# Summing two parts of a weight product's columns in the same accumulating transfers

## The chip, the cores and the metric

The kernel runs on one core of one Trainium2 chip. The metric is the time of one execution in device microseconds (us); lower is better.

## The reference, cut to what matters

Two transformer layers of width 1024 over 512 tokens. The attention halves differ; the part that matters here is the feed-forward half, which both layers have in the same shape:

```python
D_FF = -(-8 * D_MODEL // (3 * 256)) * 256        # 2816
hn = rms_norm(h, ffn_norm_g[l])
h = h + (jax.nn.silu(hn @ w_ffn_gate[l]) * (hn @ w_ffn_up[l])) @ w_ffn_down[l]
```

Everything is float32. `w_ffn_gate` and `w_ffn_up` are 1024 x 2816: 22 column tiles of 128 each.

## The kernel before, in words

Every product is done in three passes of reduced-precision matmuls: ScalarE rounds a weight tile (`wh`, the high part, `high`, L918), VectorE or GpSimd subtracts to get the rest (`wl`, the low part, L1398 and `low`, L746), and TensorE multiplies high by high, high by low and low by high (`product`, L2293).

The inner width 2816 is worked in three parts of 8, 6 and 8 column tiles (`FPARTS`). A part is first multiplied by gate and up (`gu1a`, `gu1b`, `gu1c`), then by its rows of the down weights (`dn1a` and so on); layer 2 has the same with `gu2a` to `dn2c`. In the first part four tiles of each of gate and up are plain products (`GATE_PLAIN`). All others are done in pairs of tiles with seven half products in place of eight (`tile_pair`, L2316), a scheme of the Strassen kind. Such an entry (one pair of tiles of gate, or of up) needs the weights' rows and columns in sums: four blocks of 512 rows of the weights added or copied in DRAM, `weight_sums_*`, two tensors per weight. The entries of a part are one gate and one up entry for each pair: 4 entries in part a, 6 in part b, 8 in part c.

Who makes the sums: GpSimd (POOL), in `sum_dmas`. For each layer and each part there are 16 transfers from DRAM to DRAM over the part's columns: numbers 0 to 7 are plain copies (issued at L769), 8 to 15 are accumulating ones (`accum_op=add`, L771), which read and add to what the copies left. Each transfer has 512 rows; a row is as wide as the part's pairs: 2 pairs (1024 bytes) in part a, 3 pairs (1536 bytes) in part b and 4 pairs (2048 bytes) in part c. All of them count on one semaphore, `sums_in`. In part a POOL waits only at numbers 8, 12 and 14. From part b's number 8 on (`16 * part + n >= 24`), so also at part c's copies, it waits before every transfer for all that went before, so that one is in flight at a time.

When: POOL works its own instructions in order. In layer 1 it issues part a's 16 between its `low` work for the gates (`SUMS_AT[1]`), part b's copies between the bias units of the latent attention (`mask_bias`, every fourth), and then `feed_sums` waits until the branches are mixed (`mix_ok`, L818) and issues numbers 8 to 15 of part b and all 16 of part c. In layer 2 ten of part b's 16 go between the gates, and `feed_sums` issues its other six and the 16 of part c.

Who reads them: SyncE (SP) issues the weight loads in order of use. Before the entries of a part it waits on `sums_in` for that part's sums (L672). For an entry (`load_pair`) it issues four loads: a 512 KB one of the first columns (L595, waits for `lo[0]`), a 512 KB one of a sum tensor (`wsum`, L605), a 256 KB one of the second columns (L607, waits for `lo[1]` of the entry before), and a 512 KB one of the other sum tensor (L611). All these loads have rows of 512 bytes. ScalarE then makes the high parts in its own order: `sum_high` (L1166) and `second_high` (L1172) stand in that order between the copies of the entry's partial products (`part_x`, L1226 and L1237; `part_z`), for which TensorE waits. The down tiles are loaded in two halves each (L619).

Of the kernel before, what the change touches and what calls it, by code (L numbers as in the profile page):

```python
# [39 lines left out]
FPARTS = (8, 6, 8)  # L40
# [52 lines left out]
GATE_PLAIN = (4, 0, 0)  # L93
# [15 lines left out]
def pair_list(l, part):  # L109

    return [e for i, n in gate_pairs(l, part) for e in ((i, 2 * n, False), (i + 1, 2 * n + 1, True))]
# [10 lines left out]
def first_pair(part):  # L122

    return sum(FPARTS[:part]) // 2


def tile_col(part, i):

    return (first_pair(part) + i // 2 + FPAIRS * (i % 2)) * P
# [4 lines left out]
    return i // 2 + FPARTS[part] // 2 * (i % 2)  # L134


def summed_pairs(part):

    return first_pair(part) + GATE_PLAIN[part] // 2, first_pair(part) + FPARTS[part] // 2


def down_before(l, part):
# [2 lines left out]


SUM_DMAS = 16
SUMS_AT = {1: (0, 2, 4, 6, 8, 10, 12, 14, 16), 2: (8, 10, 12, 14, 16, 19, 22, 24, 26)}


PHASES = [("kv1", 4, KD, 1), ("bq1", 2, KD, 1), ("iq1", 2, KD, 1), ("aq1", 4, KD, 2), ("uq1", 4, 2, 1),
# [150 lines left out]
def build(nc, t, out):  # L302
    with ExitStack() as ctx:
        def sem(name):
            return ctx.enter_context(nc.semaphore(name))
# [263 lines left out]
        sums_in, ws_hi, ws_lo = [sem(n) for n in "sums_in ws_hi ws_lo".split()]  # L569
# [10 lines left out]
        def by_rows(w, k0=0, kc=None):  # L580
            v = w.rearrange("(k p) n -> p k n", p=P)
            return v if kc is None else v[:, k0:k0 + kc, :]
# [5 lines left out]
        def _(sp):  # L588
            def load(name, i, b, src, col, piece=0, width=P):

                kc = KC[name]
                slot = stage[:, b, 0:kc * P].rearrange("p (k n) -> p k n", k=kc)
                if piece == 0 and not (name == "kv1" and isinstance(i, int) and i == 0):
                    sp.wait_ge(lo[b], PAIR0[name] + i)
                sp.dma_start(slot[:, :, piece:piece + width], src[:, :, bass.ds(col, width)]).then_inc(w_in[b], 16)  # L595
# [57 lines left out]
            def layer_rest(l, win, gates_at, wa, wb, wo, wg, wu, wd):  # L653
                if l == 1:
                    sp.wait_ge(lo[0], PAIR0["gates1"])
                    sp.dma_start(stage[:, 0, 0:2 * P].rearrange("p (k n) -> p k n", n=P), win[:, 0:2, gates_at:gates_at + P]).then_inc(w_in[0], 16)
                    load("gates1", 0, 1, win, gates_at + P)
                with sp.Fori(2 - l, PAIRS[f"gates{l}"]) as i:
                    for b in range(2):
                        load(f"gates{l}", i, b, win, i * (2 * P) + (gates_at + b * P))  # L660
                with sp.Fori(0, PAIRS[f"br{l}"]) as i:
                    load(f"br{l}", i, 0, by_rows(wa), i * P)
                    load(f"br{l}", i, 1, by_rows(wb), i * P)
                with sp.Fori(0, PAIRS[f"out{l}"]) as i:
                    for b in range(2):
                        load(f"out{l}", i, b, by_rows(wo), i * (2 * P) + b * P)
                for part, ab in enumerate("abc"):
                    f0 = sum(FPARTS[:part])
                    for i in range(GATE_PLAIN[part]):
                        load(f"gu{l}{ab}", i, 0, by_rows(wg), tile_col(part, i))  # L670
                        load(f"gu{l}{ab}", i, 1, by_rows(wu), tile_col(part, i))
                    sp.wait_ge(sums_in, 16 * SUM_DMAS * (3 * l - 3 + part + 1))  # L672
                    for i, q, up in pair_list(l, part):
                        load_pair(f"gu{l}{ab}", i, q, l, "u" if up else "g", first_pair(part) + (i - up) // 2)
                    with sp.Fori(0, PAIRS[f"dn{l}{ab}"]) as i:
                        for b in range(2):
                            load_down(f"dn{l}{ab}", i, b, wd, part)
# [30 lines left out]
        def _(pool):  # L708
# [40 lines left out]
                low(name, i, 0)  # L749
                low(name, i, 1)  # L750

            def sum_dmas(l, part, first, last):

                before = SUM_DMAS * (3 * l - 3 + part)
                t0, t1 = summed_pairs(part)
                cols = slice(t0 * P, t1 * P)
                second = slice((FPAIRS + t0) * P, (FPAIRS + t1) * P)
                upper, lower = slice(0, D // 2), slice(D // 2, D)
                for n in range(first, last):
                    if before + n and (n in (0, 8, 12, 14) or 16 * part + n >= 24):  # L760
                        pool.wait_ge(sums_in, 16 * (before + n))
                    m = "gu"[n % 2]
                    w, s12, s43 = w_ffn[l, m], w_sums[l, m, 0], w_sums[l, m, 1]
                    to, src = ((s12[upper, cols], w[upper, second]), (s43[lower, cols], w[upper, cols]),
                               (s12[lower, cols], w[lower, second]), (s43[upper, cols], w[lower, cols]),
                               (s12[upper, cols], w[lower, second]), (s43[lower, cols], w[upper, second]),
                               (s12[lower, cols], s43[lower, cols]), (s43[upper, cols], s12[lower, cols]))[n // 2]
                    if n < 8:
                        pool.dma_start(to, src).then_inc(sums_in, 16)  # L769
                    else:  # L770
                        pool.dma_start(to, src, accum_op=ALU.add).then_inc(sums_in, 16)  # L771

            def copies(row, dram, length, h0, h1):

                pool.dma_start(dram[:, h0:h1, 0:length], row[h0:h1].unsqueeze(0).broadcast_to([P, h1 - h0, length])).then_inc(f_out, 16)
# [18 lines left out]
            for i in range(PAIRS["gates1"]):  # L796
                if 2 <= i < 6:
                    pool.wait_ge(f_out, 16 * i)
                    windows(fB_dram, LEN_B, biasB, NKEY, 2 * i - 4, 2 * i - 2, biasB_in)
                if 1 <= i < 5:  # L800
                    copies(fB_row, fB_dram, LEN_B, 2 * i - 2, 2 * i)
                if i == 0:
                    low("gates1", i, 1)
                else:
                    low_pair("gates1", i)
                sum_dmas(1, 0, SUMS_AT[1][i], SUMS_AT[1][i + 1])

            def mask_bias(j):

# [6 lines left out]
            def feed_sums(l):  # L816

                pool.wait_ge(mix_ok, KD * l)  # L818
                sum_dmas(l, 1, 8 if l == 1 else 10, SUM_DMAS)
                sum_dmas(l, 2, 0, SUM_DMAS)  # L820

            la_units = list(latent_units())
            for b in range(2):
# [1 line left out]
            pool.wait_ge(biasB_in, 4 * 16)  # L825
            for j in range(len(la_units)):
                mask_bias(j)
                if j % 4 == 3:
                    sum_dmas(1, 1, j // 4, j // 4 + 1)

            feed_sums(1)

# [64 lines left out]
            sum_dmas(2, 0, 7, 8)  # L897
            for i in range(PAIRS["gates2"]):
                low_pair("gates2", i)
                part = SUMS_AT[2][i] // SUM_DMAS  # L900
                sum_dmas(2, part, SUMS_AT[2][i] - part * SUM_DMAS, SUMS_AT[2][i + 1] - part * SUM_DMAS)
            feed_sums(2)


# [2020 lines left out]
```

## Time and profile before

| | us |
|---|---|
| median of 3 runs (lowest, highest) | 1473.24 (1470.36, 1475.11) |
| the profiled execution's own time | 1473.38 |
| its span | 1471.7 |
| PE busy | 1452.7 (99%) |
| DVE busy / ACT busy / POOL busy | 975.2 / 654.3 / 258.2 |
| DMA queue of SP / of POOL, share of the 16 engines | 36.4% / 24.8% |

PE is TensorE's matmuls, PEld its weight loads, DVE VectorE, ACT ScalarE, POOL GpSimd, SP SyncE; a q behind a name is the engine's sequencer. The time of an execution is its span and 1.7 us around it. The granted TensorE clock is at its full 2.4 GHz level all along.

### The profile page before, as it was taken

The numbers are of one execution on the slowest core, as the hardware profiler recorded it, in microseconds if no ns is written. First come the engines' busy times: TensorE is split into PE (matmuls) and PEld (weight loads), VectorE is DVE, ScalarE is ACT, GpSimd is POOL, SyncE is SP. The second block draws the span as 40 slices with busy tenths as digits, with TensorE's granted clock in tenths as the row PEclk, the third lists the DMA queues.
The fourth block names the chain that finished last, engine by engine and source line by source line (L and its number), as shares of the span: only waits on it lengthen the run. The fifth ranks groups of instructions, "written<-read, shape, count | busy, mean of one in ns | idle before, by whom it ended". The sixth has DMA issues, their size and how long they took to land.

```text
span 1471.7 us, 23871 instructions
## 1 busy us (share of the span) xinstructions
PE 1452.7 (99%) x8712; PEld 1253.2 (85%) x8712; DVE 975.2 (66%) x1779; ACT 654.3 (44%) x1175; POOL 258.2 (18%) x260
## 2 busy tenths in 40 slices
PE   9999999999999999999999999999999999999998
PEld 8868786888898898999899777777888988989997
DVE  6678977575776576787744372434767765867875
ACT  5234446535453353465411373544344533534643
POOL 2024536201101100000003675331011001000000
PEclk9999999999999999999999999999999999999999
DMA  7536674249899993663223237653388999736632
GB/s 187 148 100 211 173 133 130 79 111 191 202 328 226 250 217 98 199 184 106 86 86 86 58 101 162 151 188 80 107 186 226 305 218 242 213 95 195 185 104 93
DMA packets 342909, 236.91 MB, mean 161 GB/s; under 512 B 24729, under 2 KB 322837, under 8 KB 342814
## 3 DMA queue, kind: packets, MB, share of 16 engines
q1 hardware_dynamic: 305518, 152.24, 36.4%
q0 software_dynamic: 37216, 83.27, 24.8%
q8 instruction: 60, 0.98, 0.3%
q14 instruction: 35, 0.29, 0.1%
q10 hardware_dynamic: 80, 0.14, 0.0%
HBM read 233.48 MB, written 81.88 MB: 214 GB/s over the span
## 4 chain that ended last, share of the span: by engine, by line
PE 88%; DMA 6%; DVE 3%; ACT 1%; issue 1%; DVEq 0%; SPq 0%; POOL 0%; ACTq 0%
PE psL L2293 37%; PE psL L2520 12%; PE psS L2316 10%; PE psL L2316 6%; PE psS L2293 5%; PE psT L2316 4%; PE psT L2529 2%; DMA stage<-in_w_ffn_up 1%; DMA stage<-in_w_ffn_gate 1%; DMA stage<-in_w_ff_up 1%; PE psL L2655 1%; PE psS L2836 1%; PE psS L2570 1%; PE psL L2791 1%; PE psS L2814 1%
## 5 line engine op out<-in xcount | busy, mean ns | idle before, releaser
L918 ACT ACTIVATE wh<-stage 128x1024 fp32r<-128x1024 f32 (+3 forms) x211 | 203.6, 965 | 362.1 <-PE psL L2293 199.6
L1398 DVE TENSOR_TENSOR wl<-stage,wh 128x1024 fp32r<-128x1024 f32 (+2 forms) x168 | 183.8, 1094 | 57.7 <-ACT wh L918 57.3
L2293 PE MATMUL psL<-hid,wh 128*128 128x512 f32 x672 | 207.3, 390 | 0.0
L2520 PE MATMUL psL<-hn,wh 128*128 128x512 f32 x496 | 165.0, 414 | 0.8 <-DVE yn L2176 0.8
L2293 PE MATMUL psL<-hn,wh 128*128 128x512 f32 x528 | 165.0, 394 | 0.0
L2293 PEld LDWEIGHTS psL<-hid,wh 128*128 128x128 f32 x672 | 125.6, 188 | 26.2 <-DVE wl L1398 0.6
L2293 PE MATMUL psL<-hid,wl 128*128 128x512 f32 x336 | 130.7, 389 | 0.0
L746 POOL TENSOR_TENSOR wl<-stage,wh 128x1024 fp32r<-128x1024 f32 (+1 forms) x43 | 97.7, 2273 | 172.7 <-ACT wh L918 172.7
L2293 PEld LDWEIGHTS psL<-hn,wh 128*128 128x128 f32 x528 | 97.7, 188 | 23.1 <-issue 3.3
L2520 PEld LDWEIGHTS psL<-hn,wh 128*128 128x128 f32 x496 | 84.5, 189 | 24.5 <-issue 11.1
L2293 PE MATMUL psL<-hn,wl 128*128 128x512 f32 x264 | 102.9, 390 | 0.0
L1901 DVE TENSOR_TENSOR wsl<-wsum,wsh 128x1024 fp32r<-128x1024 f32 x72 | 88.2, 1224 | 22.3 <-ACT wsh L1166 21.4
L2520 PE MATMUL psL<-hn,wl 128*128 128x512 f32 x248 | 97.8, 394 | 0.0
L2316 PE MATMUL psS<-xt,wsh 128*128 128x256 f32 x432 | 80.2, 283 | 0.8 <-ACT part_x L1226 0.8
L2293 PE MATMUL psL<-mix,wh 128*128 128x512 f32 x256 | 79.9, 393 | 0.8 <-DVE wl L1814 0.8
L2293 PE MATMUL psS<-hn,wh 128*128 128x264 f32 x416 | 78.5, 290 | 0.9 <-DVE hn L1845 0.5
L1166 ACT ACTIVATE wsh<-wsum 128x1024 fp32r<-128x1024 f32 x72 | 75.4, 1048 | 5.6 <-DMA wsum<-weight_sums_1g 1.9
L2293 PEld LDWEIGHTS psL<-hid,wl 128*128 128x128 f32 x336 | 63.1, 188 | 13.2
L2028 DVE TENSOR_TENSOR ft<-psL,Rk 128x512 f32<-128x512 f32 x46 | 31.8, 691 | 62.4 <-PE psL L2293 62.4
L2316 PEld LDWEIGHTS psS<-xt,wsh 128*128 128x128 f32 x432 | 67.4, 192 | 1.0 <-ACT part_x L1226 1.0
L2293 PEld LDWEIGHTS psS<-hn,wh 128*128 128x128 f32 x416 | 65.7, 192 | 2.6 <-issue 1.2
L2316 PE MATMUL psS<-xt,wsl 128*128 128x256 f32 x216 | 61.1, 283 | 0.0
(507 smaller groups left out, 3333.0 us busy)
## 6 DMA issues: line engine op xcount, KB each, us to landing
stage<-in_w_in SPq DMA_DIRECT2D x53, 512.0 KB, 4.0
wsum<-weight_sums_1g SPq DMA_DIRECT2D x18, 512.0 KB, 5.2
wsum<-weight_sums_1u SPq DMA_DIRECT2D x18, 512.0 KB, 5.3
wsum<-weight_sums_2g SPq DMA_DIRECT2D x18, 512.0 KB, 4.7
wsum<-weight_sums_2u SPq DMA_DIRECT2D x18, 512.0 KB, 4.5
stage<-in_w_out SPq DMA_DIRECT2D x16, 512.0 KB, 4.7
stage<-in_w_ffn_down SPq DMA_DIRECT2D x32, 256.0 KB, 3.0
stage<-in_w_ff_down SPq DMA_DIRECT2D x32, 256.0 KB, 3.0
```

Source lines behind the costliest of these rows:

```text
L746: pool.tensor_tensor(wl[:, b, 0:n], stage[:, b, 0:n], wh[:, b, 0:n].bitcast(F32), ALU.subtract).then_inc(lo[b], 1)
L918: act.activation(wh[:, b, 0:n], stage[:, b, 0:n], ACT.Copy).then_inc(hi[b], 1)
L1166: act.activation(wsh[:, cols], wsum[:, cols], ACT.Copy).then_inc(ws_hi, 1)
L1398: v.tensor_tensor(wl[:, b, 0:n], stage[:, b, 0:n], wh[:, b, 0:n].bitcast(F32), ALU.subtract).then_inc(lo[b], 1)
L1901: v.tensor_tensor(wsl[:, cols], wsum[:, cols], wsh[:, cols].bitcast(F32), ALU.subtract).then_inc(ws_lo, 1)
L2028: v.tensor_tensor(ft[:, 2 * b, :], psL[:, b, :], R, ALU.mult).then_inc(upper_ok, 1)
L2293: ins = pe.matmul(dst, w[:, b, k * P:(k + 1) * P], x[:, part, k, c0:c1], start=done_ + n == 0, stop=done_ == kc - 1 and n == 2)
L2316: ins = pe.matmul(dst, w[:, cols], x(part, k), start=not add and k + n == 0, stop=k == KD // 2 - 1 and n == 2, skip_group_check=True)
L2520: ins = pe.matmul(psL[:, b, :], w[:, b, k * P:(k + 1) * P], hn[:, part_, k, META:], start=k + n == 0, stop=k == KD - 1 and n == 2)
L2529: ins = pe.transpose(psT[:, n % 2, m * P:(m + 1) * P], tile[:, col:col + P], ident[:])
L2570: ins = pe.matmul(psS[:, 2 * (i % 2) + 1, h * HD:(h + 1) * HD], PTa[:, u % 2, n * P:(n + 1) * P], avn[:, c, h // 4 * HD:h // 4 * HD + HD], ...
L2655: ins = pe.matmul(psL[:, i % 2, h * HD:(h + 1) * HD], PT[:, n % 4, m * P:(m + 1) * P], vB[:, c, h * HD:(h + 1) * HD], start=h == 0 and m = ...
```

## The change

Each layer's sums are now made in two chunks instead of three: chunk 0 is part a's two pairs as before, chunk 1 is the three pairs of part b and the four of part c together, in 16 transfers whose rows are seven pairs (3584 bytes) wide. There are 32 transfers per layer instead of 48, for the same bytes. Where they stand in POOL's order changes with them: in layer 1 chunk 0's and the first two copies of chunk 1 go between the gates, the other six copies between the bias units 3, 8, 13, 18, 23 and 28, and `feed_sums` issues numbers 8 to 15; in layer 2 copies 0 to 5 go between the gates, and `feed_sums` issues copies 6 and 7 and the accumulating 8 to 15. SP waits for all of chunk 1 before part b's first entry.

```diff
+CHUNK_OF = (0, 1, 1)
+def summed_pairs(chunk):
+    parts = [n for n, c in enumerate(CHUNK_OF) if c == chunk]
+    return first_pair(parts[0]) + GATE_PLAIN[parts[0]] // 2, first_pair(parts[-1] + 1)
-SUMS_AT = {1: (0, 2, 4, 6, 8, 10, 12, 14, 16), 2: (8, 10, 12, 14, 16, 19, 22, 24, 26)}
+SUM_CHUNKS = max(CHUNK_OF) + 1
+SUMS_AT = {1: (0, 3, 6, 8, 10, 12, 14, 16, 18), 2: (8, 10, 12, 14, 16, 17, 19, 20, 22)}
+SUMS_LATER = {n: 5 * n - 7 for n in range(2, 8)}
...
-                    sp.wait_ge(sums_in, 16 * SUM_DMAS * (3 * l - 3 + part + 1))
+                    sp.wait_ge(sums_in, 16 * SUM_DMAS * (SUM_CHUNKS * (l - 1) + CHUNK_OF[part] + 1))
...
-                    if before + n and (n in (0, 8, 12, 14) or 16 * part + n >= 24):
+                    if before + n and (n in (0, 8, 12, 14) or chunk and n >= 8):
                         pool.wait_ge(sums_in, 16 * (before + n))
...
+            def sums_due(l, i):
+                for n in range(SUMS_AT[l][i], SUMS_AT[l][i + 1]):
+                    sum_dmas(l, n // SUM_DMAS, n % SUM_DMAS, n % SUM_DMAS + 1)
...
-                sum_dmas(1, 0, SUMS_AT[1][i], SUMS_AT[1][i + 1])
+                sums_due(1, i)
...
                 pool.wait_ge(mix_ok, KD * l)
-                sum_dmas(l, 1, 8 if l == 1 else 10, SUM_DMAS)
-                sum_dmas(l, 2, 0, SUM_DMAS)
+                sum_dmas(l, 1, 8 if l == 1 else 6, SUM_DMAS)
...
                 mask_bias(j)
-                if j % 4 == 3:
-                    sum_dmas(1, 1, j // 4, j // 4 + 1)
+                for n, unit in SUMS_LATER.items():
+                    if unit == j:
+                        sum_dmas(1, 1, n, n + 1)
...
-                part = SUMS_AT[2][i] // SUM_DMAS
-                sum_dmas(2, part, SUMS_AT[2][i] - part * SUM_DMAS, SUMS_AT[2][i + 1] - part * SUM_DMAS)
+                sums_due(2, i)
```

## Rows read from the trace of the kernel before

**Rows 1.** The page: engines' busy time, and the two large DMA queues.
```profile
PE 1452.7 (99%) x8712; PEld 1253.2 (85%) x8712; DVE 975.2 (66%) x1779; ACT 654.3 (44%) x1175; POOL 258.2 (18%) x260
...
q1 hardware_dynamic: 305518, 152.24, 36.4%
q0 software_dynamic: 37216, 83.27, 24.8%
```
**Rows 2.** Waits of PE's weight loads, 500 to 545 us: total, times, longest.
```profile
PEld psL L2316 <- ACT part_x L1226: 3.9, 2, 2.4
PEld psS L2316 <- ACT part_x L1226: 1.0, 1, 1.0
```
**Rows 3.** The same for 1160 to 1200 us.
```profile
PEld psL L2316 <- ACT part_x L1237: 0.7, 1, 0.7
PEld psL L2316 <- ACT part_x L1226: 0.6, 1, 0.6
PEld psT L2316 <- DVE wsl L1901: 0.6, 1, 0.6
```
**Rows 4.** Chain that ended last, from part a (layer 1) on: start, length, what.
```profile
415.85 10.07 PE psS L2316 x84
...
501.63 10.32 DMA stage<-in_w_ffn_up
...
513.36 11.18 DMA stage<-in_w_ffn_gate
...
524.56 0.64 ACT wh L1172
...
525.23 0.70 DVE wl L1906
```
**Rows 5.** POOL in order of time, layer 1: start, length [idle before, releaser].
```profile
327.69 1.05 POOL L771 DMA_DIRECT2D weight_sums_1g<-in_w_ffn_gate  x1 [60.38 <-DVE mix L1822]
...
396.07 0.66 POOL L769 DMA_DIRECT2D weight_sums_1g<-in_w_ffn_gate  x1 [8.89 <-DMA weight_sums_1u<-weight_sums_1u]
...
452.18 1.04 POOL L771 DMA_DIRECT2D weight_sums_1g<-in_w_ffn_gate  x1 [6.96 <-DMA weight_sums_1u<-in_w_ffn_up]
...
499.91 1.01 POOL L771 DMA_DIRECT2D weight_sums_1u<-weight_sums_1u  x1 [7.77 <-DMA weight_sums_1g<-weight_sums_1g]
512.05 1.01 POOL L771 DMA_DIRECT2D weight_sums_1g<-weight_sums_1g  x1 [11.12 <-DMA weight_sums_1u<-weight_sums_1u]
524.66 1.01 POOL L771 DMA_DIRECT2D weight_sums_1u<-weight_sums_1u  x1 [11.60 <-DMA weight_sums_1g<-weight_sums_1g]
```
**Rows 6.** DMA packets and queues in four stretches of 1 us: 382, 374, 508 and 512.
```profile
DMA packets 128, 0.20 MB, mean 197 GB/s; under 512 B 0, under 2 KB 128, under 8 KB 128
...
DMA packets 206, 0.21 MB, mean 210 GB/s; under 512 B 0, under 2 KB 206, under 8 KB 206
...
DMA packets 165, 0.21 MB, mean 209 GB/s; under 512 B 0, under 2 KB 84, under 8 KB 165
...
DMA packets 683, 0.35 MB, mean 348 GB/s; under 512 B 4, under 2 KB 683, under 8 KB 683
```
**Rows 7.** SP in order of time, layer 1: start, length.
```profile
408.60 0.37 SPq L607 DMA_DIRECT2D stage<-in_w_ffn_gate  x1
...
443.04 38.71 SPq L619 DMA_DIRECT2D stage<-in_w_ffn_down  x16
486.17 0.38 SPq L595 DMA_DIRECT2D stage<-in_w_ffn_gate  x1
```
**Rows 8.** The load issued at 417.33 and the one at 370.07: KB, us to landing.
```profile
stage<-in_w_ffn_up SPq DMA_DIRECT2D x1, 256.0 KB, 7.2
...
stage<-in_w_ffn_gate SPq DMA_DIRECT2D x1, 512.0 KB, 8.2
```
**Rows 9.** POOL in order of time, layer 2.
```profile
1068.59 1.00 POOL L771 DMA_DIRECT2D weight_sums_2g<-in_w_ff_gate  x1 [52.39 <-DVE mix L1822]
...
1174.54 1.04 POOL L771 DMA_DIRECT2D weight_sums_2g<-in_w_ff_gate  x1 [7.38 <-DMA weight_sums_2u<-in_w_ff_up]
```
**Rows 10.** SP in order of time, layer 2.
```profile
1148.43 0.37 SPq L607 DMA_DIRECT2D stage<-in_w_ff_gate  x1
...
1229.15 0.38 SPq L595 DMA_DIRECT2D stage<-in_w_ff_gate  x1
```
**Rows 11.** The copy of part b's sums issued at 239.08: KB, us to landing.
```profile
weight_sums_1g<-in_w_ffn_gate POOLq DMA_DIRECT2D x1, 768.0 KB, 4.6
```

More of the change, by code:

```diff
@@ L134, in hid_slot @@
     return i // 2 + FPARTS[part] // 2 * (i % 2)
-def summed_pairs(part):
-    return first_pair(part) + GATE_PLAIN[part] // 2, first_pair(part) + FPARTS[part] // 2
+CHUNK_OF = (0, 1, 1)
+def summed_pairs(chunk):
+    parts = [n for n, c in enumerate(CHUNK_OF) if c == chunk]
+    return first_pair(parts[0]) + GATE_PLAIN[parts[0]] // 2, first_pair(parts[-1] + 1)
 def down_before(l, part):
@@ L750, in low_pair, with sum_dmas @@
                 low(name, i, 1)
-            def sum_dmas(l, part, first, last):
-                before = SUM_DMAS * (3 * l - 3 + part)
-                t0, t1 = summed_pairs(part)
+            def sum_dmas(l, chunk, first, last):
+                before = SUM_DMAS * (SUM_CHUNKS * (l - 1) + chunk)
+                t0, t1 = summed_pairs(chunk)
                 cols = slice(t0 * P, t1 * P)
```

## The prediction

> **What bounds the kernel now.** I read the page first: PE is busy 99% of the span [rows 1], so a transfer matters only where PE waits for what it brings, and the whole idle time of PE is 1471.7 - 1452.7 = 19.0 us. Then I asked for the waits of PE's weight loads in the stretches of the feed-forward parts. Late weights cost PE something in two places: 3.9 + 1.0 = 4.9 us in layer 1 between 500 and 545 us, in part b [rows 2], and 0.7 + 0.6 + 0.6 = 1.9 us in layer 2 between 1160 and 1200 us, in part a [rows 3]. Part a of layer 1, part b of layer 2 and both parts c have none worth naming. So 6.8 us is all that the change can win from the transfers it merges.
>
> Why the 4.9 us arise is to be seen by laying the chain beside POOL's order. The second loads of three entries are issued at 501.63, 513.36 and 525.95, each 1.3 to 1.7 us after an accumulating transfer of four pairs (499.91, 512.05, 524.66), and take 10.3, 11.2 and 10.2 us, as long as that transfer [rows 4, 5]. The high and the low part follow (0.64 and 0.70 us), and only then does the next entry's second load go out. So an entry took as long as an accumulate, about 12.0 us, where PE needs 10.07 [rows 4]. The packets in single microseconds tell why a load waits [rows 6]: with no accumulate active the loads move 683 packets of 512 bytes in 1 us; beside an accumulate of four pairs they move 84 to its 81, and beside one of three pairs (206 packets, 210 GB/s, which solves to 104 to 102) again one to one. Alone, rows of three pairs go at 128 in 1 us.
>
> **The change, part by part.**
>
> The accumulates. 128 rows of 1536 bytes in 1 us over 16 engines is 125 ns a row and engine; a load packet in between adds 16/683 us = 23 ns. A transfer of 512 rows is 32 per engine: three pairs 32 x (125 + 23) = 4.7 us of active time, four pairs 32 x (167 + 23) = 6.1 us, seven pairs 32 x (292 + 23) = 10.1 us, an estimate that scales the row by its bytes. The rest of a transfer's period is latency at both ends in which loads run freely. In the feed-forward stretch the periods before are (396.07 - 327.69)/8 = 8.5 us for three pairs, and 12.0 us for four pairs beside entries [rows 5]. Seven pairs then take 8.5 + 5.4 = 13.9 us beside plain tiles and 12.0 + 4.0 = 16.0 us beside entries. Bounds from rows: at least 8.5 us a transfer (if width cost nothing), at most 8.5 x 7/3 = 19.9 us (if all of it grows with the bytes).
>
> When they run. Layer 1: from 327.69 on, five at 13.9 reach 397, three at 16.0 end at 445. Before, the three-pair ones ended at 396, copies of four pairs ran to 452.18 and the four-pair accumulates from there to 536 [rows 5]. So part b loses its accumulates and its 4.9 us stall goes; but part a, whose loads go out from 403 to 443 [rows 7], now meets accumulates with the long active time where it met copies. Layer 2: from 1068.59 [rows 9] two copies of seven pairs, 14 us as an estimate from two of 4.6 us at three pairs [rows 11] scaled by 7/3 with loads between them, little of it overlapped, then five at 13.9 to 1152 and three at 16.0 to 1200. Part a's second loads go out from 1148.43 on [rows 10], so its four entries lie under the fifth to the eighth.
>
> What one costs part a. An entry's four loads are 1.75 MB, 3584 packets. In a period of 16.0 us the loads get 512 packets in the active 10.1 us and 683 x 5.9 = 4030 outside it: 4540, good for 1.27 entries or 12.7 us of PE. That is a loss of 3.3 us each at the least, if the loads use every gap. If the entries lock to the accumulates as they did in part b before, one entry goes with each: a loss of 16.0 - 10.1 = 5.9 us. I take the middle, 4.6. Against it stands the slack at part a: the load issued at 417.33 took 7.2 us [rows 8] and was there at 424.5, and ACT needs it about 1 us behind the entry's start at 425.9 (the first start at 415.85 and one entry more), so about 2.5 us, spent once in each layer. The accumulate that covers the first entry is absorbed by SP's lead, since that entry's loads go out 7 us ahead of it. Layer 1: 2 x 4.6 - 2.5 = 6.7 (4.1 to 9.3). Layer 2: 3 x 4.6 - 2.5 = 11.3 (7.4 to 15.2).
>
> Plain tiles (out, and the first of gate and up). A load issued just behind a three-pair accumulate takes 8.2 us [rows 8] with no stall; with seven pairs it is 8.2 + 5.4 = 13.6 us. A load can be issued about three tiles ahead of its use (5.4 us each), less rounding and subtracting twice: some 11.7 us. Only a load in the first 2 us of a transfer can be late, one in three. I take 0, with 2.4 us a layer as the other end.
>
> The wait moved at L672. SP comes to it when the down loads of part a are out, at 443.04 + 38.71 = 481.8, and its next load goes at 486.17 [rows 7]; chunk 1 is there at 445. In layer 2 the load is at 1229.15 [rows 10] and the chunk at 1200. 0 us; behind this wait stand all of part b's loads, so it is the dearest place if the chunk is late (a rival below).
>
> POOL. Sixteen issues less per layer. In the attention phases two issues of 0.63 us fewer stand between the bias units; PE's own work ends the waits there, so 0. The wider copies there run beside few loads; the 60 us [rows 5] for which POOL then idles is their cover. Copies between the gates: same cover. If that were gone, a copy's extra 3 us would have to be seen in a gate tile's load, which has two tiles' time.
>
> Sum: 1473.4 + 6.7 + 11.3 - 4.9 - 1.9 = 1484.6 us, against a profiled time that is the median of the runs within 0.2 us.
>
> Two rules of the Trainium skill bear on this, both on its page "DMA: Bandwidth & Descriptors". The rows show packets of the two queues alternating one to one [rows 6]; the section "Queues, rings and completion order" says that an engine takes turns between queues by packets, whatever a packet holds, which speaks against wide rows beside narrow ones, and by it the sum stands as above. The section "Anatomy of one DMA — SWDGE (gpsimd) path" gives 2.0 us fixed and the bytes at 436 GB/s, by which 1.8 MB would take 6.2 us and merging would be a clear gain; the trace does not agree for accumulates, whose rows move at 197 GB/s when alone [rows 6].
>
> **Rivals.**
>
> A, faster: the accumulates need not grow so much, the gaps carry part a's loads, and the stalls of before go. For it: nothing is in flight beside part b any more, and part a of layer 1 had no stall. Against it: one-to-one packets. If seven pairs took 8.5 to 12 us each, no entry would be late: 1473.4 - 6.8 = 1466.6 us; with a us or two left in each layer 1468.
>
> B, no change: the entries' stalls only move from part b to part a, about 3 us in each layer, since the loads catch up in gaps and slack is larger than I read: 1473 us, 1470 to 1477.
>
> C, slower by another way: chunk 1 is late at SP's wait. It decides from 19.9 us a transfer on: layer 1 would end at 327.7 + 159 = 487, 1 us late and covered, layer 2 at 1068.6 + 14 + 159 = 1242, 12.5 us behind 1229.15, of which some 7 are covered by SP's lead. That is 6 us on top of part a's loss at its upper ends (9.3 + 15.2 + 4.8 - 6.8 = 22.5): 1501 us.
>
> **How the numbers follow.** Forecast (part a pays, 1478 to 1496) 0.5; A 0.22; B 0.2; C 0.08. The forecast's own range is the lower bounds, 1473.4 + 11.5 - 6.8 = 1478, to the upper, 1496. For the range of 8 in 10 I go down to 1467, which takes in B and most of A, and up to 1495. A measurement of this kernel tells 0.3%, 4.4 us, from no change. Faster: A, with a little of B, 0.24. Same: most of B and the edges of its neighbours, 0.22. Slower: 0.54.
>
> **What would show it.** Right: accumulates of chunk 1 with periods of about 14 and then 16 us, ending near 445 (later by the stalls) and 1200; PE waiting for `part_x` in part a of both layers, 6.7 and 11.3 us; load packets at some 50 in 1 us while one is active; no waits left in layer 1's part b. Wrong: periods under 12 us, or part a without stalls, which gives A; a gap in SP behind the last down load of part a, which gives C. PE waits in the out and plain tiles would show the term that I set to 0.

## The result and the profile after

| | before | after |
|---|---|---|
| median of 4 runs (lowest, highest), us | 1471.8 (1467.6, 1475.1) | 1517.1 (1515.1, 1519.5) |
| span of the profiled execution | 1471.7 | 1517.8 |
| PE busy / PE idle in the span | 1452.7 / 19.0 | 1468.9 / 48.9 |
| mean granted clock | 0.997 | 0.986 |

The changed kernel takes 1.0308 times as long (95% interval 1.0283 to 1.0334): slower, as forecast, but by 45 us where 11 were forecast, and outside the range.

The page after, the lines that answer to [rows 1]:
```profile
PE 1468.9 (97%) x8712; PEld 1262.9 (83%) x8712; DVE 977.8 (64%) x1779; ACT 655.9 (43%) x1175; POOL 231.8 (15%) x228
q1 hardware_dynamic: 305518, 152.24, 35.1%
q0 software_dynamic: 25696, 83.27, 22.9%
```
The same 8712 matmuls now take 16.2 us more, so part of the loss is the clock, and PE stands still 29.9 us more. Both DMA queues move the same bytes as before.

The difference lies in few stages. I cut the spans where PE's first matmul of each stage starts and asked for the busy time in each. Columns of a row: stretch, its length, then busy time of PE, PEld, DVE, ACT, POOL, and at the end the granted clock, the DMA share and GB/s. Before, plain tiles (out, first gate and up) and part a's entries of layer 1, part b's entries, then plain tiles and part a of layer 2:
```profile
326.10:415.70 89.60, 89.60 (x395) 73.11 (x396) 62.06 (x88) 40.55 (x53) 10.67 (x12) 1.00 0.92 210
415.70:456.00 40.30, 40.30 (x338) 40.30 (x336) 30.12 (x42) 22.59 (x39) 3.55 (x5) 1.00 0.96 297
499.60:566.50 66.90, 62.69 (x506) 62.08 (x504) 46.48 (x63) 33.84 (x58) 3.04 (x3) 0.97 0.84 211
1067.00:1156.60 89.60, 89.60 (x394) 73.09 (x395) 62.27 (x88) 40.45 (x53) 9.89 (x12) 1.00 0.89 227
1156.60:1199.00 42.40, 41.17 (x338) 40.53 (x338) 29.87 (x42) 22.25 (x38) 4.33 (x5) 1.00 1.00 257
```
After, the same five:
```profile
325.90:433.20 107.30, 96.62 (x394) 76.76 (x395) 61.88 (x88) 40.85 (x53) 8.11 (x8) 0.94 1.01 212
433.20:480.30 47.10, 43.03 (x338) 42.80 (x337) 30.91 (x43) 22.81 (x39) 0.00 (x0) 0.93 0.63 176
523.80:584.30 60.50, 60.50 (x505) 60.46 (x505) 47.22 (x63) 34.19 (x58) 0.00 (x0) 1.00 0.58 166
1084.60:1192.80 108.20, 95.87 (x395) 75.98 (x396) 61.52 (x88) 40.75 (x53) 8.38 (x9) 0.95 0.99 226
1192.80:1245.10 52.30, 43.63 (x337) 43.23 (x336) 31.03 (x43) 22.71 (x39) 1.00 (x1) 0.93 0.76 195
```
| us, after less before | layer 1 | layer 2 | forecast |
|---|---|---|---|
| plain tiles | +17.7 | +18.6 | 0, 0 |
| part a's entries | +6.8 | +9.9 | +6.7, +11.3 - 1.9 |
| part b's entries | -6.4 | 0.0 | -4.9, 0 |

These sum to 46.6 us, against 46.1 between the spans; part a's and part b's down tiles and all of part c agree within 0.2 us. Of the first plain term 10.7 us are PE standing still (107.3 - 96.6) and 7.0 us the same matmuls at a lower clock (96.6 - 89.6). Two single microseconds of that stretch, the first inside a wait and the second with PE busy all along:
```profile
345.00:346.00 1.00, 0.11 (x1) 0.12 (x1) 1.00 (x2) 0.00 (x0) 0.00 (x0) 0.50 0.93 161
415.00:416.00 1.00, 1.00 (x4) 0.81 (x3) 1.00 (x2) 0.43 (x1) 0.00 (x0) 0.50 1.05 208
```
0.50 is the 1.2 GHz level; before, no stretch of these stages but 516 to 520 us showed it, inside part b of layer 1 and right behind one of its waits. So, other than the section on the profile before says, the granted clock was not at its full level all along: part b's mean of 0.97 in the row above is this dip, and two more of 3 to 5 us lie outside these stages.

The accumulates themselves came as forecast. POOL in order of time, [rows 5] and [rows 9] of before:
```profile
327.53 1.04 POOL L777 DMA_DIRECT2D weight_sums_1g<-in_w_ffn_gate  x1 [60.89 <-DVE mix L1832]
342.69 1.01 POOL L777 DMA_DIRECT2D weight_sums_1u<-in_w_ffn_up  x1 [14.12 <-DMA weight_sums_1g<-in_w_ffn_gate]
...
396.19 1.01 POOL L777 DMA_DIRECT2D weight_sums_1u<-weight_sums_1u  x1 [13.02 <-DMA weight_sums_1g<-weight_sums_1g]
410.01 1.01 POOL L777 DMA_DIRECT2D weight_sums_1g<-weight_sums_1g  x1 [12.81 <-DMA weight_sums_1u<-weight_sums_1u]
423.44 1.01 POOL L777 DMA_DIRECT2D weight_sums_1u<-weight_sums_1u  x1 [12.42 <-DMA weight_sums_1g<-weight_sums_1g]
```
The seven periods lie between 13.0 and 15.2 us (13.9 forecast). What PE waits for in the plain tiles of layer 1, 320 to 433 us (total, times, longest):
```profile
PEld psL L2303 <- DVE wl L1408: 12.1, 6, 3.6
```
`wl` is the low part of a weight tile. Why it is late stands in the chain that ended last, here through the plain tiles:
```profile
372.07 10.87 DMA stage<-in_w_ffn_up
...
382.97 1.07 ACT wh L928
...
384.06 1.24 DVE wl L1408
...
385.31 11.52 DMA stage<-in_w_ffn_up
...
399.27 11.54 DMA stage<-in_w_ffn_up
...
413.25 10.73 DMA stage<-in_w_ffn_up
```
There is no PE in this chain at all. One weight buffer goes round: a load of 11 us beside an accumulate, 1.07 us of rounding, 1.24 of subtracting, and only then, the buffer being free, the next load into it. A round takes 13.2 to 14.0 us, the accumulate's period, and feeds two tiles (there are two buffers), for which PE needs 10.9 us. Each of these four loads goes out 3.1 to 3.2 us behind an accumulate's issue and lands 1.0 to 1.1 us behind that accumulate's landing (381.88, 395.82, 409.73 and 422.88 us). The loads into the other buffer go out later in the transfer and take 6.3 to 8.1 us; they are not in the chain.

The packets in single microseconds, for [rows 6]: 338 to 339 us with loads beside the accumulate, 374 to 375 without.
```profile
DMA packets 105, 0.22 MB, mean 217 GB/s; under 512 B 0, under 2 KB 52, under 8 KB 105
...
DMA packets 60, 0.22 MB, mean 215 GB/s; under 512 B 0, under 2 KB 0, under 8 KB 60
```
52 load packets to 53 of the accumulate: still one to one, the forecast's "some 50". This also says why a load lands with the accumulate, worked out from the counts and not tested by itself: a load of 512 KB is 1024 packets, an accumulate has 512 rows, so beside one accumulate at most half of the load gets through, and the rest goes when it has ended. Part b's first load goes out at 510.47 behind the last down loads at 499.67, as before; SP does not wait for the chunk, whose last transfer landed at 436.7.

### The profile page after: what moved, and what is told of

Same layout as the page of the kernel before. It is cut to its first block, busy times and chain, and to the rows that moved or that the text cites. A ratio compares the mean times of both kernels' runs of the same rounds, so it can differ in the third digit from the quotient of the medians.

```text
span 1517.8 us, 23838 instructions
## 1 busy us (share of the span) xinstructions
PE 1468.9 (97%) x8712; PEld 1262.9 (83%) x8712; DVE 977.8 (64%) x1779; ACT 655.9 (43%) x1175; POOL 231.8 (15%) x228
## 4 chain that ended last, share of the span: by engine, by line
PE 80%; DMA 12%; DVE 4%; ACT 2%; issue 1%; POOL 0%; DVEq 0%; ACTq 0%; SPq 0%; POOLq 0%
PE psL L2303 27%; PE psL L2530 12%; PE psS L2326 11%; PE psL L2326 7%; PE psT L2326 5%; PE psS L2303 5%; DMA stage<-in_w_ff_up 4%; DMA stage<-in_w_out 4%; DMA stage<-in_w_ffn_up 3%; PE psT L2539 2%; DVE wl L1408 1%; PE psS L2846 1%; PE psL L2665 1%; ACT wh L928 1%; PE psS L2580 1%
## 5 line engine op out<-in xcount | busy, mean ns | idle before, releaser
L2303 PE MATMUL psL<-hn,wh 128*128 128x512 f32 x528 | 169.2, 402 | 10.7 <-DVE st L1929 8.1
L2530 PE MATMUL psL<-hn,wh 128*128 128x512 f32 x496 | 165.0, 414 | 0.8 <-DVE yn L2186 0.8
L2303 PE MATMUL psL<-hn,wl 128*128 128x512 f32 x264 | 104.4, 395 | 0.0
L2303 PE MATMUL psL<-mix,wh 128*128 128x512 f32 x256 | 84.6, 413 | 11.3 <-DVE wl L1408 10.9
L2303 PEld LDWEIGHTS psL<-hid,wl 128*128 128x128 f32 x336 | 63.1, 188 | 13.2
L2303 PEld LDWEIGHTS psL<-mix,wh 128*128 128x128 f32 x256 | 49.9, 199 | 25.9 <-DVE wl L1408 13.1
## 6 DMA issues: line engine op xcount, KB each, us to landing
weight_sums_1g<-in_w_ffn_gate POOLq DMA_DIRECT2D x6, 1792.0 KB, 10.3
weight_sums_2u<-in_w_ff_up POOLq DMA_DIRECT2D x6, 1792.0 KB, 11.3
```

Source lines behind the costliest of these rows:

```text
L2303: ins = pe.matmul(dst, w[:, b, k * P:(k + 1) * P], x[:, part, k, c0:c1], start=done_ + n == 0, stop=done_ == kc - 1 and n == 2)
L2530: ins = pe.matmul(psL[:, b, :], w[:, b, k * P:(k + 1) * P], hn[:, part_, k, META:], start=k + n == 0, stop=k == KD - 1 and n == 2)
```

## The experiments

Stage lengths are from one profiled execution each. They are given as plain tiles | part a | its down tiles | part b | its down tiles; with nothing late they are 89.6 | 40.3 | 43.5 | 60.5 | 32.8 us.

**No adding.** All of chunk 1's transfers plain copies (the sums lack their second terms): `pool.dma_start(to, src)` without `accum_op` at L777.

> The change with the accumulating transfers as plain copies of the same rows, so the sums are left without their second terms. Theory L, which puts the cost on how slowly an accumulate's rows drain (197 GB/s): copies of four pairs moved at over 350 GB/s, so seven pairs are active some 5 us, the period is about 8 us, no loss anywhere: 1466 us (1463 to 1470). Rival W (wide rows alone starve the loads, add or not): 1490 us or more.

Measured 1472.3 us, ratio 0.9998 (0.9978 to 1.0018), 2 us above the range that was expected. Layer 1 has 89.6 | 40.3 | 43.5 | 60.5, with seven-pair copies every 8.2 to 10.0 us; layer 2 has 96.6 | 40.9, PE waiting 5.2 us once behind the two wide copies that its `feed_sums` issues together. So rows seven pairs wide do no harm as copies one at a time, which rules out the rival (wide rows alone); it is the accumulating that is slow. The miss is the two copies in flight together in layer 2.

**Narrower accumulates, one chunk.** Each accumulate of chunk 1 is cut by columns into two, worked one behind the other (the same bytes, the same order, SP's wait as changed):
```
for c0, c1, done in ((0, first * P, cut_in), (first * P, 7 * P, sums_in)):
    pool.dma_start(to[:, c0:c1], src[:, c0:c1], accum_op=ALU.add).then_inc(done, 16)
```
with `first` 3, 5 and 6.

> The change with each accumulate of chunk 1 as two, of three and then of four pairs; copies, their places and the wait of SP stay merged. Theory L: periods of 8.5 and some 10.5 us, both under 10.9, no loss in the plain tiles; the last ends near 327.5 + 8 x 19 = 480, about when SP comes to the wait; 2 to 4 us lost in part a: 1472 us (1467 to 1478). Theory S (the loss comes from the merged schedule, that is from adding seven pairs where three were added before, not from the length of one transfer): 1500 us or more.

> The change with each accumulate of chunk 1 as one of five and one of two pairs. Between the splits 3 and 4 (nothing lost in layer 1's plain tiles) and 6 and 1 (5.3 us lost). Theory L: five pairs are active 32 x (208 + 23) ns = 7.4 us, a period of some 11.2 us, round 10.9 us at most: 0 to 1.5 us lost in layer 1's plain tiles: 1486 us (1481 to 1493). Rival (the loss grows with the count or the bytes alone): the same as 3 and 4 or as 6 and 1, 1481 or 1501 us.

> The same, of six pairs and then of one. Theory L: six pairs are active 8.8 us, a period of 12.2 us, 1.3 us over PE's two tiles, once in 18.7 us: some five times a layer in the plain tiles, 6 us, and 3 us in part a with the clock's share: 1487 us (1480 to 1497). Theory S: as the change or later, 1517 us.

| widest piece, pairs | us (ratio, interval) | plain tiles, layer 1 | part a, layer 1 |
|---|---|---|---|
| 4 | 1481.2 (1.0055, 1.0030 to 1.0080) | 89.8 | 47.5 |
| 5 | 1487.6 (1.0108, 1.0076 to 1.0140) | 92.4 | 45.1 |
| 6 | 1501.0 (1.0175, 1.0131 to 1.0218) | 95.0 | 48.6 |
| 7 (after) | 1517.1 (1.0308, 1.0283 to 1.0334) | 107.3 | 47.1 |

Only the five-pair version came inside its expected range; the other two lay 3 and 4 us above theirs, the four-pair one because part a lost 7 us where 2 to 4 were expected. With four pairs the plain tiles of layer 1 lose 0.2 us though the chunk takes longer in all; the loss rises with the width of one transfer, from between four and five pairs on. Part a pays at any width, since more of chunk 1 now lies beside it. In layer 2 the plain tiles of the four-pair version take 98.1, 8.5 us too long, close to the 7.0 us that the version without adding lost there to the two wide copies.

**Sums laid out by tiles.** The sum tensors as `[pair, row, 128]` in place of `[row, pairs * 128]`, and so seven runs of 512 bytes per row on the accumulate's side.

> The change with the sums kept tile by tile in DRAM, so that every row of a sum transfer is 512 bytes, as a load's is; as many transfers, as many bytes. Theory L (a load is held because its packets alternate one to one with the accumulate's wide rows, and a stage buffer goes round in flight + 2.3 us, so PE loses where that exceeds its 10.9 us for two tiles): 32 x 7 rows per engine at 42 + 23 ns make 14.6 us active and a period of 18 us, longer than the 13.4 us of the change, but the loads get 245 packets a us in it where plain tiles need 188. No loss in the plain tiles, some 3 us in each part a: 1472 us (1466 to 1480). Theory P (the time an accumulate is in flight is what costs, whatever its rows): 7 us lost for each of five accumulates a layer, 1540 us or more.

Measured 1528.3 us, ratio 1.0376 (1.0332 to 1.0421); layer 1 has 96.5 | 53.3 | 45.3 | 60.5, layer 2 95.1 | 51.4 | 55.3 | 62.4. The hope for short packets failed, and 1528 us lies with neither theory: POOL needs 4.5 us for one issue, the periods are 21 to 27 us, and the mix of layer 1 is reached 9 us later (335.3).
```profile
337.05 4.53 POOL L784 DMA_DIRECT2D weight_sums_1g<-in_w_ffn_gate  x1 [55.46 <-DVE mix L1839]
361.68 4.48 POOL L784 DMA_DIRECT2D weight_sums_1u<-in_w_ffn_up  x1 [20.10 <-DMA weight_sums_1g<-in_w_ffn_gate]
```
Longer issue, longer transfers and shorter rows changed together here, so the run does not tell whether the turns by packets or the length of the transfer holds the loads. It shows what rival C would have been, in layer 2: SP at L601 waits 16.2 us for the last of chunk 1, and PE 11.6 us for the loads behind it.
```profile
SPq L601 <- DMA weight_sums_2u<-weight_sums_2u: 16.2, 1, 16.2
...
PEld psS L2333 <- DVE wl L1415: 11.6, 1, 11.6
```

**The wide copies of layer 2 early.** Copies 6 and 7 go between the gates: `SUMS_AT[2] = (8, 10, 12, 14, 16, 18, 20, 22, 24)`; layer 1 is untouched.

> The change with layer 2's copies 6 and 7 of chunk 1 issued between the gates, so that feed_sums has only the eight accumulates in both layers. Theory L: the two wide copies together hold loads for once (6.9 us lost in layer 2's out and gate tiles where the accumulates were plain copies), so layer 2's plain tiles lose some 4 us less: 1512 us (1508 to 1516). Rival: the copies hide behind the accumulates' own loss and nothing changes, 1517 us.

Measured 1505.6 us, ratio 1.0236 (1.0204 to 1.0269). Layer 2 has 103.9 | 46.9, 4.2 and 5.5 us less than after (108.1 | 52.4 by the same cut), and the time is 2 us below the expected range: a gain for one line. But layer 1, the same program, has 102.7 where after has 107.3. So I ran the changed kernel once more.

> The changed kernel itself once more, on this call's chip. The kernel with the layer 2 copies moved had the same program in layer 1 and yet took 102.7 us there against 107.3 for the plain tiles, with loads of 10.4 us against 11.5 beside an accumulate. If the time of such a load differs between chips or executions, this run's plain tiles of layer 1 lie anywhere from 102 to 108 us and its loads from 10.3 to 11.6; if the two kernels really differ there, 107 again. Time 1505 to 1520 us.

Measured 1515.5 us, ratio 1.0289 (1.0254 to 1.0325), as expected, with 104.4 | 46.7 in layer 1 and 105.9 | 52.2 in layer 2. A stage length of a stalled kernel is thus good to some 3 to 5 us only: the same program lost 17.7, 14.8 and 13.1 us in layer 1's plain tiles. In layer 2 the early copies gain 2.0 to 4.2 us in the plain tiles, which is within that, and 5.3 to 5.5 us in part a, in both comparisons: without the two copies ahead of them the accumulates are through part a sooner.

**Accumulates spaced out.** As the version with the copies early, but each accumulate of chunk 1 waits for PE's progress. They start 14 to 28 us apart in layer 1, five of them in the plain tiles and three in part a.

> The same, with the eight seven-pair accumulates of each layer released by TensorE's progress, one to every 3 or 4 tiles (16 to 22 us) in place of one right behind the other (13.4 us). Theory L in its form of a loop (a stage buffer goes round in flight + 2.35 us, and only when accumulates follow each other does every second tile's load meet one; a lead once lost is won back in a gap): plain tiles lose 0 to 2 us a layer where the change lost 17.7 and 18.5; part a still 5 a layer: 1478 us (1472 to 1484). Rival E (every long accumulate costs PE its 3 to 4 us wherever it stands): 1505 us or more.

Measured 1520.9 us, ratio 1.0333 (1.0300 to 1.0367): 96.9 | 58.0 | 45.8 in layer 1 and 100.0 | 57.3 | 45.8 in layer 2. My theory, that only accumulates back to back cost anything because the loads' lead recovers between them, fell, and the time lies where the rival had it. Five accumulates in the plain tiles cost 7.3 and 10.4 us (1.5 and 2.1 each), three in part a 17.7 and 17.0 (5.9 and 5.7 each); already the first load beside one, at the mix, took
```profile
332.37 11.91 DMA stage<-in_w_out
```
and PE was late for it.

**One accumulate at a time.** All real accumulates are left out (the sums lack terms), the copies are early, and one accumulate into an unused tensor is released in each stage, seven pairs wide in layer 1 and four in layer 2: `pool.dma_start(aux[0:D // 2, 0:width], ..., accum_op=ALU.add)`.

> The changed kernel's copies stand, all its sixteen real accumulates of the two layers are left out (the sums lack their second terms), and six lone accumulates a layer into a tensor that nobody reads are released one at a time by TensorE's or VectorE's progress: behind the mix, in the first and in a middle entry of part a, in its down tiles, in part b's entries, in its down tiles, in part c's entries; seven pairs wide in layer 1, four pairs wide in layer 2. Theory (a load that shares an accumulate's active time is late by what its flight exceeds its own lead, and one accumulate costs that once): seven pairs, each: plain tiles 0 to 2.6 us (flight 12 to 13.6 us against a lead that the spaced kernel showed to be 9.6 to 11), part a 2.5 to 5.9, down tiles 0 to 3 (halves of 256 KB, long lead), part b 3 to 5.9, part c 3 to 5.9; four pairs, each: 0 in plain tiles, 0 to 1.9 in part a, b and c, 0 in down tiles. Layer 1 then has 90 | 44 | 44 | 65 | 33 to 36 us for plain tiles, part a, its down tiles, part b, its down tiles, layer 2 89.6 | 41 | 43.5 | 61 | 32.8. Rival (only a run of accumulates back to back costs anything, since the loads' lead recovers in between): 89.6 | 40.3 | 43.5 | 60.5 | 32.8 in both layers. Time 1478 to 1488 by the theory, 1467 by the rival.

Measured 1488.1 us (2 runs), ratio 1.0108 (1.0078 to 1.0138). Layer 1, plain tiles to part c, seven pairs:
```profile
326.30:417.10 90.80, 89.75 (x395) 72.97 (x396) 62.29 (x88) 40.55 (x53) 1.04 (x1) 1.00 0.48 128
417.10:463.20 46.10, 41.97 (x337) 41.77 (x336) 30.75 (x42) 22.77 (x39) 1.03 (x1) 0.96 0.72 184
463.20:507.10 43.90, 43.90 (x195) 36.03 (x194) 22.76 (x27) 10.59 (x11) 1.01 (x1) 1.00 0.61 153
507.10:572.10 65.00, 62.19 (x506) 61.99 (x504) 47.10 (x63) 34.20 (x58) 1.01 (x1) 0.97 0.69 183
572.10:610.10 38.00, 34.59 (x146) 27.99 (x145) 20.80 (x27) 9.03 (x11) 1.00 (x1) 0.96 0.62 149
610.10:695.00 84.90, 82.45 (x674) 82.21 (x674) 64.24 (x85) 47.41 (x78) 1.01 (x1) 0.98 0.71 192
```
Against 89.6, 40.3, 43.5, 60.5, 32.8 and 80.6 a single seven-pair accumulate costs 1.2, 5.8, 0.4, 4.5, 5.2 and 4.3 us. Four pairs cost 0, 0.2, 0.1, 0, 0.6 and 0 in layer 2. Of the 5.8 us, 4.1 are a wait and 1.7 the clock that falls behind it (0.61 from 436 to 440 us). The two beside down tiles differ by 4.8 us for the same width, and the longest down load took the same in both, 10.3 us in part a's down tiles (the cheap one) and 10.5 in part b's. What differs is PE: it needs 10.9 us for two of part a's down tiles (43.5 for eight) and 8.2 for two of part b's (32.8 for eight). That accounts for 2.7 of the 3.4 us that it waits in the dearer one; the other 1.8 of the 5.2 us are the clock. It fits the rule, but no run varied it alone. The expectation missed for the dearer one and held for the other seven-pair ones.

**Only the first accumulates.** Early copies, and of chunk 1's accumulates only three in layer 1 and five in layer 2, back to back from the mix on (the sums lack terms).

> The changed kernel with the seven-pair copies of layer 2 all between the gates, and with only the first three accumulates of chunk 1 in layer 1 and the first five in layer 2, back to back behind the mix; the others are left out (the sums lack terms), so part a meets none. Theory (while accumulates run back to back, a weight buffer's round is one accumulate's flight and the 2.35 us of rounding and subtracting, against 10.9 us that PE takes for the two tiles; so each accumulate costs its period less 10.9 us, some 2.3 us, and the first one the 1.2 us that a lone one cost): plain tiles 1.2 + 2 x 2.3 = +5.8 us in layer 1 (95.4) and 1.2 + 4 x 2.3 = +10.4 in layer 2 (100.0), part a 40.3 to 41 in both. Rival (the loads' lead of 11.7 us takes up the first accumulates and only the later ones cost): 90 to 92 in layer 1, 93 to 96 in layer 2. Time: before less its 6.4 and 2.0 us of waits, plus these: 1480 us by the theory, 1470 by the rival.

Measured 1481.0 us, ratio 1.0063 (1.0039 to 1.0087).
```profile
326.30:423.10 96.80, 91.74 (x395) 74.27 (x396) 62.02 (x88) 40.75 (x53) 3.07 (x3) 0.98 0.66 157
423.10:463.40 40.30, 40.30 (x338) 40.30 (x337) 30.85 (x42) 22.85 (x39) 0.00 (x0) 1.00 0.57 166
1066.20:1167.40 101.20, 92.47 (x394) 73.99 (x395) 61.95 (x88) 41.09 (x53) 5.11 (x5) 0.98 0.83 186
1167.40:1207.80 40.40, 40.40 (x338) 40.36 (x338) 30.86 (x42) 22.95 (x39) 0.00 (x0) 1.00 0.57 165
```
The theory had 95.4 and 100.0, 1.4 and 1.2 us less; the rival, that the lead takes up the first accumulates, is out. Three cost 7.2 us and five 11.6: 2.4 and 2.3 us each, close to the period (12.9 to 13.5 us, but for the first, 14.7 and 15.8) less the 10.9 us of two tiles, and nothing is recovered between them. That the first of a run costs as much as the next is not shown: the single one in the same place cost 1.2. After's plain tiles hold seven of them and most of the eighth, at 2.3 us some 17 to 18, which is the missing term (17.7 and 18.6 measured; the two other executions of layer 1's program had 14.8 and 13.1).

**Part c's last accumulates later, three chunks.** The kernel before, with the last three of part c held until part b's down tiles:
```
sum_dmas(l, 2, 0, 13)
pool.wait_ge(lo[0], PAIR0[f"dn{l}b"] + 1)
sum_dmas(l, 2, 13, SUM_DMAS)
```


> The kernel before with one pause: part c's last three accumulates wait until part b's loads are out (the first down tile of part b), so that they lie beside down tiles and not beside part b's entries. Theory L: the 4.9 us that layer 1's part b waits go, and what the clock adds; part c's sums are there by 587, before SP comes for them at 590: 1466 us (1463 to 1470), faster than the kernel before. Rival: the wait for the sums takes their place, 1472 us or more.

Measured 1473.6 us, ratio 1.0013 (0.9991 to 1.0036). Part b loses its 6.4 us, and part a of layer 2 has 40.3; but the down tiles of part b take 35.4 and 39.5 in place of 32.8, and those of part a in layer 2 44.9. A down tile of part b takes 4.1 us of PE, two of them 8.2, and the accumulates there have a period of 9.3 us in layer 1: the same rule with other numbers gives 1.1 us each, which covers its 2.6 us. Layer 2's 6.7 us are more than it gives, and stay open in part (2.3 us of them are the clock). So the expected 1466 us did not come, though the stall in part b went as expected: the accumulates took their price from the down tiles.
```profile
566.25 1.01 POOL L771 DMA_DIRECT2D weight_sums_1g<-weight_sums_1g  x1 [8.31 <-DMA weight_sums_1u<-weight_sums_1u]
575.64 1.01 POOL L771 DMA_DIRECT2D weight_sums_1u<-weight_sums_1u  x1 [8.38 <-DMA weight_sums_1g<-weight_sums_1g]
```

**Wide copies, narrow accumulates, each where it fits.** Copies seven pairs wide and early, part b's accumulates of three pairs behind the mix on a semaphore `b_in` of their own (SP waits for them before part b), part c's of four pairs: one, then five while SP loads part a's down tiles, the last two, in pieces of two pairs, while it loads part b's.
```
for n in range(8, 16):
    add(l, n, 0, 3, b_in)
...
    if n == 9:
        pool.wait_ge(lo[1], PAIR0[f"dn{l}a"])
    if n == 14:
        pool.wait_ge(lo[1], PAIR0[f"dn{l}b"])
```


> All sums are made and the result is the reference's. The seven-pair copies are all issued ahead of the mix in both layers, where the loads are few; the accumulates are cut back to three pairs (part b's eight, right behind the mix, on a semaphore of their own, for which SP waits ahead of part b) and four pairs (part c's: one, then a pause until part a's last second load has been rounded, five beside part a's down tiles, a pause until part b's last entry, the last two beside its down tiles, each in two pieces of two pairs). Theory (an accumulate costs by its width and by the slack of the loads beside it; copies early cost nothing): part b of layer 1 loses the 6.4 us it waits or runs at the low clock before, part a of layer 2 its 2.0, down tiles pay 0 to 1.5 us a layer: 1463 to 1466 us, ratio 0.994 to 0.996. Rival (the accumulates' cost is the same wherever they stand, as the kernel with part c's last three paused showed for part b's down tiles): 1471 to 1475 us.

Measured 1466.8 us (12 runs), ratio 0.9962 (0.9946 to 0.9978): 0.4% faster than the kernel before and 3% faster than the changed one, 0.8 us above what the theory expected. Early copies, narrow accumulates and their places changed together, so their shares are not told apart; beside part b's down loads the paused version had three whole accumulates, this one two in halves. Part a and its down tiles, part b and its down tiles of layer 1, and part a of layer 2:
```profile
419.30:459.60 40.30, 40.30 (x337) 40.30 (x336) 30.85 (x42) 22.82 (x39) 1.01 (x1) 1.00 0.73 188
459.60:503.10 43.50, 43.50 (x194) 36.03 (x193) 23.03 (x27) 10.67 (x11) 4.05 (x4) 1.00 0.95 206
503.10:563.60 60.50, 60.50 (x505) 60.46 (x505) 47.21 (x63) 34.18 (x58) 2.02 (x2) 1.00 0.65 179
563.60:596.40 32.80, 32.80 (x146) 26.98 (x145) 20.80 (x27) 9.06 (x11) 2.02 (x2) 1.00 0.76 165
...
1155.30:1195.60 40.30, 40.30 (x337) 40.30 (x336) 30.84 (x42) 22.89 (x39) 1.10 (x2) 1.00 0.73 190
```
PE never waits in these stages; the plain tiles of layer 1, not shown, have 90.1 where 89.6 is the least. Of the 8.4 us so won (6.4 and 2.0) the median shows 6.1; the profiled execution reached the mix of layer 1 3 us later than before (329.1 against 326.1), and I have not traced what of that is the wide copies and what the execution.

## Why the prediction was wrong

**The step that failed** is "Plain tiles ... I take 0, with 2.4 us a layer as the other end". It measured 17.7 and 18.6 us, 36 of the 46. The prediction compared a load's 13.6 us with 11.7 us, the lead from a load's issue to its use with everything on time, and concluded that only a load in the first 2 us of a transfer can be late, one in three. Two things were wrong in that. A load's lead counts once; in a run of accumulates the condition is the round of one buffer, load plus 2.35 us of rounding and subtracting against 10.9 us for two tiles. That leaves a load 8.6 us. And the round ties itself to the accumulate's period: the loads in the chain went out 3.1 to 3.2 us behind the accumulate, outside those 2 us, and still took 10.7 to 11.5 us, because they landed with it. So every accumulate holds one such load, which is every second load, and each round costs the period less 10.9 us. At [rows 8]'s 8.2 us beside three pairs the round is 10.55 us, 0.35 us under the limit, and I read the absence of stalls there as slack. Another load of the kernel before, issued at 386.73, was over it with no stall in its stage:
```profile
stage<-in_w_ffn_up SPq DMA_DIRECT2D x1, 512.0 KB, 9.2
```
so the limit holds for a run of such loads and not for a single one. From the forecast's own period, 13.9 - 10.9 = 3.0 us times seven would have given 21 us a layer, against 17.7 measured. The versions cut to four, five and six pairs (0.2, 2.8, 5.4 us) and the one with three and five accumulates alone (2.4 and 2.3 us each) show that the cost goes with the length of one accumulate and with their number; that it is the buffer's round that passes it on to PE is read from the chain, which has no PE in it.

**The clock** was left out. PE's busy time grew by 16.2 us. Where the buffer's round sets the pace, I take it to be no loss of its own (by the chain the round fixes the sum, whether PE idles or runs slowly), which no run shows by itself; in the entries it comes on top: 2.7 us in part a of layer 1 (43.0 against 40.3), 2.5 in layer 2 (43.6 against 41.2). That it follows the waits is shown by the single accumulates: the four that made PE wait 2.4 us or more had a dip right behind, the two others none. That waits cause it is argued, since nothing was run that changes the clock alone. (The Trainium skill, page "TensorE: Matmul & The Clock Gate", section "Part 1: The HAM clock gate (the "warmup" mystery)", says that how busy PE has been sets the gate; the dips agree.)

**Part a.** 6.8 and 9.9 us against 6.7 and 9.4 forecast net: the sizes are right by luck. Forecast were accumulates beside part a that cost 4.6 us each, less 2.5 us of slack: two of them in layer 1 and three in layer 2, and none for the one that covers the first entry, "absorbed by SP's lead". But the stretched plain tiles took nearly all of them in. In layer 1 none was issued in part a, and the last one, of 423.44, met only the loads of the first two entries. The first entry's second load went out at 426.42, 6.8 us ahead of the entries, took 11.4 us, and PE waited for it:
```profile
PEld psS L2326 <- ACT part_x L1236: 4.3, 1, 4.3
```
So the term that was put at nothing made all of the wait. In layer 2 one was issued in part a (1197.91), and PE waited 4.8 and 4.3 us. PE stood still for 4.1 us (47.1 - 43.0) in layer 1 and 8.7 in layer 2; the rest is the clock. The price itself, 4.6 us, was too low: a single one cost 5.8 us (4.1 + 1.7), the spaced ones 5.9 and 5.7, at the forecast's upper end.

**What held.** Periods near 13.9 us beside plain tiles; packets one to one whatever their size; part b's stall gone (6.4 us where 4.9 were counted: 4.2 us of PE idle, 66.9 - 62.7, and 2.2 of the clock, which was at 0.97 over part b before); no wait at the moved line, with chunk 1 done near 437 in layer 1, long before SP comes there. (The Trainium skill, page "DMA: Bandwidth & Descriptors", section "Queues, rings and completion order", says that an engine takes turns between queues by packets; the counts of 52 to 53 agree. The 2.0 us and 436 GB/s of the same page's section "Anatomy of one DMA — SWDGE (gpsimd) path" do not fit the accumulates: by them 1.8 MB would take 6.2 us, an estimate, where the single one behind the mix took 12.6 us from issue to landing.) One thing more was left out and cost something: the two wide copies at the head of layer 2's `feed_sums`, to whose 14 us I had given no price beside the loads (5.2 us of wait in the version without adding). In the change they took 17.5 us, from 1086.29 to the next issue at 1103.83.

**The rivals.** A and B are out: the periods were 13.0 to 15.2 us where A wanted 8.5 to 12, and the loss was 45 us where B had none. C's place stayed free in the change and was met only by the layout by tiles. One question stays open: an accumulate reads and writes DRAM beside the loads, and no run separates what the loads lose to the turns by packets from what they may lose there.

## What to carry to other kernels

With two buffers, ask of a run of slower transfers not whether one load still arrives in time but whether flight plus conversion is below the engine's time for the two tiles that a round feeds; above it, every transfer of the run costs about the difference. Ask also how many packets a load has against the rows of the transfer beside it: here a load had twice as many, and the loads in the chain landed 1 us behind it. What merging costs then goes by the length of one transfer: seven-pair copies, one at a time, cost the neighbours nothing, while accumulates cost nothing or 0.2 us up to four pairs in the plain tiles and more from five on. A stage without stalls does not say how near it is to the limit.

## What was not expected of the hardware

- A transfer that accumulates from DRAM to DRAM moved 197 to 215 GB/s alone, three or seven pairs wide; plain copies of the same shape had periods of 8.2 to 10.0 us where the accumulates had 13 to 15.
- The cost of one accumulate jumps with width: four pairs 0 to 0.6 us in every stage, seven pairs 4.3 to 5.8 us in four of six (1.2 and 0.4 in the others). The widths stood in different layers.
- An accumulate whose destination is seven runs of 512 bytes for each row kept GpSimd for 4.5 us at its issue, against 1.0 us for one run of 3584 bytes, and its period rose from 14 to between 21 and 27 us.
- Behind waits of 2.4 to 4.1 us, one in a stage, the granted clock stood at the 1.2 GHz level for several microseconds; in the changed kernel the same matmuls took 16 us more in all.
